# Hybrid decoder layer on one core: stick-breaking sticks alternate between two heads, values' product on two column tiles

## What is computed

```python
z = jnp.einsum('bhqd,bhkd->bhqk', qb, kb) * scale
mask = s_idx[None, :] < t_idx[:, None]
log_beta = jax.nn.log_sigmoid(z)
log_1m = jnp.where(mask, log_beta - z, 0.0)
log_a = log_beta + lax.cumsum(log_1m, axis=3, reverse=True) - log_1m
A = jnp.where(mask, jnp.exp(log_a), 0.0)
outs.append(jnp.einsum('bhqk,bhkd->bhqd', A, vb))
```

## Time and profile before

| | |
|---|---|
| median of 3 executions | 1752.62 us (1748.5 to 1753.45) |
| the profiled execution | 1744.41 us, of which the profile's span is 1742.4 us |
| PE busy | 1588.2 us (91%) |
| DVE, ACT, POOL busy | 825.1, 704.8, 510.0 us |
| mix stage, by the trace | about 390 to 862 us of the span |

### The profile page before, as it was taken

One profiled execution on the slowest core, in us unless ns is written; L12 is line 12 of the kernel. 1 busy time (PEld: TensorE's weight loads), 2 busy tenths in 40 slices (PEclk: granted clock), 3 DMA queues, 4 the chain that ended last, 5 costly groups with the idle time before them and its releaser, 6 DMA issues. The chain is left out here.

```text
span 1742.4 us, 37310 instructions
## 1 busy us (share of the span) xinstructions
PE 1588.2 (91%) x15220; PEld 1305.3 (75%) x15220; DVE 825.1 (47%) x1125; ACT 704.8 (40%) x1239; POOL 510.0 (29%) x523
## 2 busy tenths in 40 slices
PE   4999999967999989888928969999999999999997
PEld 3999999965666666666507848888888888888886
DVE  5132442426566665666592433444444444444436
ACT  5243534516667676677633433222222222222213
POOL 6332432413444444344343532111111111111110
PEclk7999999989999999999969979999999999999999
DMA  3334364373413232111232232111111111111104
GB/s 136 109 128 163 122 213 164 122 207 83 106 45 79 51 82 48 45 31 38 62 85 85 97 120 73 49 49 48 48 48 48 48 48 48 48 48 48 60 1 169
DMA packets 79517, 143.91 MB, mean 83 GB/s; under 512 B 15632, under 2 KB 51472, under 8 KB 79392
## 3 DMA queue, kind: packets, MB, share of 16 engines
q1 hardware_dynamic: 75648, 128.26, 23.9%
q10 hardware_dynamic: 3744, 13.85, 2.0%
HBM read 104.51 MB, written 37.57 MB: 82 GB/s over the span
## 5 line engine op out<-in xcount | busy, mean ns | idle before, releaser
L1793 POOL TENSOR_TENSOR ffn_ul<-ffn_relu,ffn_uh 128x512 fp32r<-128x512 f32 x64 | 82.8, 1293 | 575.3 <-ACT ffn_uh L1765 575.3
L1822 DVE TENSOR_TENSOR all_acc<-all_acc,ffn_down 128x512 f32<-128x512 f32 x240 | 161.1, 685 | 121.8 <-PE ffn_down L1869 121.3
L618 PE MATMUL inproj_acc<-xn_xh,inproj_wh 128*128 128x346 f32 (+1 forms) x624 | 207.3, 332 | 8.4 <-DVE inproj_wl L539 8.4
L1861 PE MATMUL ffn_up<-all_mh,ffn_wuh 128*128 128x512 f32 x512 | 200.2, 391 | 10.9 <-DVE ffn_wul L1805 10.9
L618 PE MATMUL inproj_acc<-xn_xh,inproj_wl 128*128 128x346 f32 (+1 forms) x624 | 201.0, 322 | 0.0
L618 PE MATMUL inproj_acc<-xn_xl,inproj_wh 128*128 128x346 f32 (+1 forms) x624 | 200.8, 322 | 0.0
L1861 PE MATMUL ffn_up<-all_mh,ffn_wul 128*128 128x512 f32 x512 | 199.9, 390 | 0.0
L1861 PE MATMUL ffn_up<-all_ml,ffn_wuh 128*128 128x512 f32 x512 | 199.9, 390 | 0.0
L1869 PE MATMUL ffn_down<-ffn_wdh,ffn_uh 128*128 128x512 f32 x512 | 199.7, 390 | 0.0
L1869 PE MATMUL ffn_down<-ffn_wdh,ffn_ul 128*128 128x512 f32 x512 | 199.4, 389 | 0.0
L1869 PE MATMUL ffn_down<-ffn_wdl,ffn_uh 128*128 128x512 f32 x512 | 199.2, 389 | 0.0
(11 more groups left out here) (249 smaller groups left out, 3444.4 us busy)
## 6 DMA issues: line engine op xcount, KB each, us to landing
ffn_raw_u<-in_w_up SPq DMA_DIRECT2D x32, 512.0 KB, 3.3
ffn_raw_d<-in_w_down SPq DMA_DIRECT2D x32, 512.0 KB, 4.2
xn_raw<-in_w_in SPq DMA_DIRECT2D x28, 512.0 KB, 4.5
p_scratch<-inproj_out ACTq DMA_DIRECT2D x26, 520.0 KB, 2.7
chunk_scratch<-inproj_fields SPq DMA_DIRECT2D x4, 2720.0 KB, 9.2
mix_swp<-chunk_scratch SPq DMA_DIRECT2D x68, 128.0 KB, 3.7
inproj_rkv<-p_scratch SPq DMA_DIRECT2D x14, 520.0 KB, 4.6
mix_fld<-chunk_scratch SPq DMA_DIRECT2D x17, 256.0 KB, 3.0
```

What stands on the lines that cost most here:

```text
L618: last = pe.matmul(acc[g][:, 0:size], w[s][:, kt, :], xx[:, kt, col:col + size], start=(kt == 0 and j == 0), stop=(kt == KD - 1 and j == 2))
L1793: pool.tensor_tensor(ul[s][:, f, cols], relu[j % 2][:, :], uh[s][:, f, cols].bitcast(F32), ALU.subtract).then_inc(u_low.sem, 1)
L1822: dve.tensor_tensor(part, part, downs[o % 4][:, :], ALU.add).then_inc(added.sem, 1)
L1861: last = pe.matmul(ups[j][:, :], w[f][:, k, :], xx[:, k, cols], start=(k == 0 and jj == 0), stop=(k == KD - 1 and jj == 2))
```

## The change

- **Order of tasks.** The loop over the two heads is now innermost: block b of head 0, then of head 1. Each head has its own bank for the running sum (`cbs[h]`); the second `zb` bank is given up for it. Scores of task t now wait for the copy of task t-1 (`z_copied`), no longer t-2.
- **Quarters.** PE's order in a tick is scores, rest, values' product, tri; tri runs for t = now - 3. ACT's is exp and ln of t = now - 1, weights of now - 5, copy of z of t = now, then output copy and splits. DVE's is the difference of now - 4, splits, the max of now - 1, the clamp of now. POOL works on now - 1.
- **Values' product.** Made once for both heads of a block, at the second head's tick, in pieces of 128 queries; each piece is two products with a 128x64 stationary operand, one into rows 0 to 63 of `ob`, one into rows 64 to 127. The output copy is one 128x512 copy for both heads.
- **Buffers.** `w` 5 to 3, with two extra 128x128 tiles `wn` for the narrow tasks; `a` 3 to 4.
- **Loads and splits.** By part instead of by head: part 0 is queries 512 up and keys 640 up of both heads, part 1 the rest (`load_part`, `PARTS`, `K_EDGE`). The number of transfers is the same.

```diff
+PARTS = 2
+K_EDGE = (SBW // P + 1) * P
...
-        for h in range(2):
-            for g in reversed(range(GROUPS)):
-                for b in range((g + 1) * SBW // P, -1, -1):
-                    if n in TURN_BEFORE and i + 1 < PAIRS:
-                        ticks.append(Turn(i + 1, TURN_BEFORE.index(n)))
+        for g in reversed(range(GROUPS)):
+            for b in range((g + 1) * SBW // P, -1, -1):
+                if n in TURN_BEFORE and i + 1 < PAIRS:
+                    ticks.append(Turn(i + 1, TURN_BEFORE.index(n)))
+                for h in range(2):
                     ticks.append(Task(i, h, g, b))
                     n += 1
...
-        w = [m.sb(f"w{i}", [P, SBW]) for i in range(5)]
+        w = [m.sb(f"w{i}", [P, SBW]) for i in range(3)]
+        wn = [m.sb(f"wn{h}", [P, P]) for h in range(2)]
...
-        a = [m.sb(f"a{i}", [P, SBW]) for i in range(3)]
-        zb = [m.ps(f"zb{i}") for i in range(2)]
-        cb = m.ps("cb")
+        a = [m.sb(f"a{i}", [P, SBW]) for i in range(4)]
+        zb = m.ps("zb")
+        cbs = [m.ps(f"cb{h}") for h in range(2)]
...
+                    t = now - 1
+                        clamped.wait(act, t)
+                        act.activation(part, part, ACT.Exp).then_inc(exp_done.sem, 1)
+                        exp_done.wait(act, t)
+                        act.activation(part, part, ACT.Ln, bias=1.0).then_inc(ln_done.sem, 1)
+                    yield
+                    t = now - 5
...
+                    t = now
                         z_done.wait(act, t)
                         exponent.wait(act, t - 4)
-                        act.activation(z[t % 4][:, off:], zb[t % 2][:, off:], ACT.Copy, scale=HD ** -0.5).then_inc(z_copied.sem, 1)
+                        act.activation(z[t % 4][:, off:], zb[:, off:], ACT.Copy, scale=HD ** -0.5).then_inc(z_copied.sem, 1)
...
-                        act.activation(o_sb[half, i, g * SBW:(g + 1) * SBW], ob[half, :], ACT.Copy).then_inc(o_copied.sem, 1)
+                        act.activation(o_sb[:, i, g * SBW:(g + 1) * SBW], ob[:, :], ACT.Copy).then_inc(o_copied.sem, 1)
...
-                        z_copied.wait(pe, t - 2)
+                        z_copied.wait(pe, t - 1)
...
-                        pe.matmul(ob[:, off:], v[i % 2][:, b, :], a[t % 3][:, off:], start=first, stop=at(t).last,
-                                  skip_group_check=True).then_inc(pv_done.sem, 1)
+                        for c in range(off, SBW, P):
+                            for h in range(2):
+                                half = slice(h * HD, (h + 1) * HD)
+                                last = pe.matmul(ob[half, c:c + P], v[i % 2][:, b, half], a[(t - 1 + h) % 4][:, c:c + P], start=first,
+                                                 stop=at(t).last, skip_group_check=True)
+                        last.then_inc(pv_done.sem, 1)
+                    yield
+                    t = now - 3
+                    if is_task(t):
+                        soft_low.wait(pe, t)
+                        sums(tri, tri_r, t, at(t).first).then_inc(tri_done.sem, 1)
```

More of the change, by code:

```diff
@@ L895, in _, with before_diagonal @@
             pool.tensor_copy(rest_r[:, :], rest[:, :]).then_inc(tri_set, 1)
[L897 to L898 removed]
+            def before_diagonal(columns, marks):
+                part = columns[:, 0:P]
                 pool.affine_select(out=part, in_=part, compare_op=ALU.is_gt, fill=0.0, base=0,
@@ L911, in _ @@
                     if at(t).diag:
-                        before_diagonal(w[t % 5], off, soft_masked)
+                        before_diagonal(soft_of(t), soft_masked)
                         soft_masked.wait(pool, t)
-                    if SBW - off >= 2 * P:
-                        part, high, low = (x[:, off:] for x in (w[t % 5], wsh[t % 4], wsl[t % 4]))
+                    if not at(t).narrow:
+                        part, high, low = soft_of(t), wsh[t % 4][:, off:], wsl[t % 4][:, off:]
                         rest_done.wait(pool, t - 4)
+                        tri_done.wait(pool, t - 4)
                         pool.tensor_copy(high, part).then_inc(soft_high.sem, 1)
@@ L991, in sticks @@
                     if is_task(t):
+                        part = w[t % 3][:, at(t).off:]
+                        clamped.wait(act, t)
[5 more added lines that the diff above has]
+                    if is_task(t):
+                        part = a[t % 4][:, at(t).off:]
+                        exponent.wait(act, t)
+                        act.activation(part, part, ACT.Exp).then_inc(weights.sem, 1)
+                    yield
+                    t = now
+                    if is_task(t):
                         off = at(t).off
@@ L1020, in sticks @@
                         high_k(*split_at[now - 1])
-                    yield
-                    t = now - 5
-                    if is_task(t):
-                        part = a[t % 3][:, at(t).off:]
-                        exponent.wait(act, t)
-                        act.activation(part, part, ACT.Exp).then_inc(weights.sem, 1)
                     yield
@@ L1312, in sticks @@
                     t = now - 5
-                    if is_task(t):
+                    if is_task(t) and not at(t).last:
                         exponent.wait(pe, t)
-                        if at(t).last:
-                            pe.sem_inc(rest_done.sem, 1)
-                        else:
-                            sums(rest, rest_r, t, at(t).off, False).then_inc(rest_done.sem, 1)
-                    yield
-                    t = now - 4
-                    if is_task(t):
-                        soft_low.wait(pe, t)
-                        sums(tri, tri_r, t, at(t).off, at(t).first).then_inc(tri_done.sem, 1)
+                        sums(rest, rest_r, t, False).then_inc(rest_done.sem, 1)
                     yield
                     t = now - 6
-                    if is_task(t):
+                    if t in second_ticks:
                         i, b, off, first = at(t).i, at(t).b, at(t).off, at(t).first
-                        (weights_masked if at(t).diag else weights).wait(pe, t)
+                        for x in (t - 1, t):
+                            (weights_masked if at(x).diag else weights).wait(pe, x)
                         if first:
```

141 lines of the change are left out of this document (75 added, 66 removed).

## The result

| | before | changed |
|---|---|---|
| median | 1752.06 us (4 runs, 1748.5 to 1753.45) | 1725.17 us (4 runs, 1724.79 to 1725.99) |
| profiled execution, its span | 1744.41, 1742.4 us | 1725.34, 1723.6 us |
| mix stage, us of the span | 390 to 860.3 | 390 to 841 |
| PE busy in it, PE idle in it | 416.40, 53.9 us | 394.66, 56.3 us |

The ratio is 0.9859 [0.9839, 0.9878], -26.9 us where -36 was forecast; between the two profiled executions it is -19.1 (that of before was the fastest of its kernel). The difference of the two spans lies in the mix stage: its ends in the table are 19.3 us apart; what lies behind it takes 1742.4 - 860.3 = 882.1 us before and 1723.6 - 841 = 882.6 after. The table's last row tells where the gain is: PE works 21.7 us less, and is idle no less than before.

The account below looks back on a forecast made before the run. PE was taken as the bound in work, yet idle 54 us in the 472 us mix stage. -31 - 30 + 25 = -36 us: profiled execution 1744.4 to 1708.4, median 1752.6 to 1716.6; range 1683 to 1758.

Parts of the forecast that it names:

- First term: PE's values' product on two column tiles: 46 us instead of 84, plus 7 for tiling changes, -31 us.
- the rival at 1748.6: Values' product: the two column tiles don't overlap, so its term is +11 and the total -4 us; chance 0.19.
- the 70 tiling changes: PE's array switches between full and tiled products 354 times instead of 284, at a mean of 0.1 us: +7 us.
- Second term: Two running-sum banks: PE's waits of `rest` (26.7 us) and before the output copy (3.9 us) go, -30 us.
- the last sentence of the prediction: If PE idles as before and the stage is only 30 us shorter, the two-bank gain was given back: right for wrong reason.
- Third term: One scores bank: PE's scores wait for ACT's copy, held up by exp waiting for the clamp, +25 us.
- an upper bound of 73: One scores bank's greatest cost to PE: 31 us of exposed clamps plus 42 for clamps held up by POOL.
- that ACT did not stand before: ACT's exp directly behind the copy waits for its own task's clamp in 51 of 112 cases: 31 us of new standing.
- The edits at nothing: Stick instructions, fewer `w` buffers, loads and splits cost nothing; tick 0's second split is covered, otherwise a few us once.
- PE alone as the bound: Mix stage: ACT's new waits fit its slack, so the scores bank costs 0: -61 us, 1691.6; chance 0.14.
- The slow ring of the clamp: ACT, DVE and POOL go round one ring, 4.4 us a tick; with all 64 wide ticks +22 us, 1774.6; chance 0.17.
- The slow side: The whole kernel gets slower by more than 5.3 us: chance 0.16, against 0.70 faster and 0.14 the same.

Follow-up runs that it names:

- e2: Changed kernel with the values' product in one piece per head, up to 512 queries, instead of pieces of 128: 1723.94 us, ratio 0.987.
- e3: Changed kernel with all 128-query pieces of head 0 first, then all of head 1, instead of alternating: 1736.24 us, ratio 0.9926.
- e12: Kernel before, one sum bank, PE's order scores, values' product, rest, tri; DVE takes the difference first and the clamp last: 1786.68 us, ratio 1.0221.
- e9: Changed kernel with one more PE wait: tri of task t also waits for the difference of t-1: 1728.95 us, ratio 0.9896.
- e4: Changed kernel without DVE's clamp, exp reading z itself (the minimum with 40 left out): 1711.62 us, ratio 0.9789.
- e5: Kernel before without DVE's clamp, exp reading z itself (the minimum with 40 left out): 1733.74 us, ratio 0.9914.
- e6: Changed kernel with ACT's weights of now - 5 ahead of exp and ln of now - 1: 1727.16 us, ratio 0.9885.
- e8: Changed kernel with ACT's copy of z first in the tick, ahead of exp, ln and weights: 1731.87 us, ratio 0.9897.
- e7: Changed kernel with the first pair's second split at tick 6 and ACT's weights ahead of exp and ln: 1722.55 us, ratio 0.9846.
- e10: Changed kernel with ACT's copy of z first in the tick and the first pair's second split at tick 6: 1727.29 us, ratio 0.9877.
- e1: Changed kernel with the first pair's second split called for at tick 6 instead of tick 0: 1724.28 us, ratio 0.9868.
- e11: Changed kernel run again as it is, on another chip: 1726.13 us, ratio 0.9861.

## Why the prediction was right, and where not

**First term, -31: right in size.** The groups cost 32 x 1.03 + 8 x (0.37 + 0.59 + 0.81) = 47.1 us (0.59 from a 256 wide group, 0.81 on the line between), where 46 were forecast and 84 stood before. The reason given, column tiles that overlap as the slot's tiles do, holds: e2's trace shows records of two products that start and end together, and e3 takes part of the overlap away by order alone and loses 12 us. The Trainium skill's rule ("TensorE: Matmul & The Clock Gate", Part 3, The mechanism), that a load is hidden only behind matmuls of other row groups, would have made a group of 512 cost about 8 x 0.25 = 2.0 us, an estimate from the earlier trace rows. It takes 1.03, so the rule as the prediction quotes it doesn't hold for these 128x64 tiles. The same section leaves a second way open, a load into the background weight buffer; no run here tells whether that is how it goes. This was the rival at 1748.6, and it is out.

PE's busy time fell by only 21.7 us, though. The products alone account for 84 - 47.1 = 37, so some 15 us of other work came in. 7 of them were forecast, for the 70 tiling changes. About 4 are clock, by an estimate from the rows of the first 30 us: 17.88 us at 0.64 lose 6.4 us against full speed, 21.46 us at 0.89 lose 2.4. The 4 or so that remain no run took apart (behind 420 us the clock is 0.99 instead of 1.00), nor was the price of a tiling change measured after.

**Second term, -30: the waits went, the time didn't.** The 26.7 us of `rest` and the 3.9 us before the output copy are gone as said. But PE's idle time of the stage is 56.3 us against 53.9, where 54 - 30 + 25 = 49 was forecast. This is the case that the last sentence of the prediction named: right for the wrong reason, as far as the second bank goes. The rows of PE's waits say where the time went: the scores' waits for the one bank brought back 25.2 + 2.2 = 27.4 us, as the third term had it, the turns at the start 7.9, and the other rows nearly cancel. The reason for the second term holds only in part. e12 brings `rest` down to 6.8 us with one bank, and in e9 the wait that one bank would add for the next tri costs 2.4. As far as these two runs go, it was the places in the tick more than the second bank; the tick of slack for `rest` could not be tested by itself.

**Third term, +25: the size right, with luck, and its cause not borne out.** PE waits 25.2 + 2.2 us for the one scores bank. The 25 was a third of an upper bound of 73, whose parts were all prices of the clamp. One reading under it was wrong: the median of 428 ns over all clamps mixes four widths, and does not say that a 512 wide clamp was unhindered; of these, 14 of 64 took over 1 us before, and 7 after. The chain from POOL over the clamp to exp to the copy does occur; DVE's, ACT's and PE's timelines show one:

```profile
556.96 1.29 POOL L936 TENSOR_TENSOR mix_wsl<-mix_w,mix_wsh 128x512 fp32r<-128x512 f32 x1
```

```profile
557.24 1.30 DVE L1149 TENSOR_SCALAR mix_w<-mix_z 128x512 f32<-128x512 f32 x1 [1.03 <-ACT mix_z L1026]
```

```profile
558.57 0.63 ACT L1011 ACTIVATE mix_w<-mix_w 128x512 f32<-128x512 f32 x1 [1.36 <-DVE mix_w L1149]
...
560.76 0.59 ACT L1026 ACTIVATE mix_z<-mix_zb 128x512 f32<-128x512 f32 x1
```

```profile
561.41 0.50 PE L1322 MATMUL mix_zb<-mix_qh,mix_ks 128*128 128x512 f32 x1 [0.79 <-ACT mix_z L1026]
```

The clamp began at 557.24 beside POOL's low part (556.96 + 1.29 = 558.25) and took 1.30 us; exp stood 1.36 us for it, the copy ended at 560.76 + 0.59 = 561.35, and the scores had stood 0.79 us. The rule of the Trainium skill on the shared ports ("SBUF — State Buffer", Who interferes with whom) fits in kind, as with the earlier trace rows: the clamp is held up until POOL's part ends. It isn't met to the letter, since the clamp ended 558.54 - 558.25 = 0.29 us behind POOL's part, in the earlier trace rows 0.15, where a 512 wide one takes 0.43 unhindered; times on POOL are rough. But this is not what sets the total. The clamp of 512 takes 615 ns on the mean in both kernels; without it both orders gain, 12 us (e4) and 15 us (e5); and with half of ACT's wait removed and the clamps shorter (e6), PE waits as long as in the changed kernel. The step that failed here is "that ACT did not stand before": ACT stood 61.0 us at its copies, behind the difference. The change moved these waits to exp (65.4), and e8 moves them back to the copy (101.4). Which resource sets the pace of this ring (POOL's two parts, DVE's three operations, the 4 buffers of z, or the scores bank) stays open. More z buffers were not tried, nor a second scores bank beside the two sum banks.

**The edits at nothing: this step failed.** "The second is now called for in tick 0, which PE's and ACT's wait for the first chunk covers": it doesn't. ACT stood 6.89 us for the second load, the first copy of z came 5.4 us later than before, and PE's turns waited 7.9 us. With the split at tick 6 the first copy is early again in all three traces, and the medians are 4.6 us lower twice (e7 under e6, e10 under e8), though e1 alone doesn't show it. The low clock at the start is not the split's doing alone: it was 0.64 here, but 0.73 in e1 and 0.56 in e7. The prediction had named the price of a missing cover, "a few us once", and then not put it into the sum.

That makes half of the 9 us between forecast and result in the medians. Held against the traces, from which the sum was made, the forecast is further off: 1708.4 against 1725.34, 17 us. Of these, 9 are PE's work (-21.7 where -31 was forecast) and 7 its idle time (+2.4 where -5 was), in which the turns' 7.9 us lie. That the medians are nearer is luck: the profiled execution of before was its fastest, 8 us under the median.

**The other rivals.** PE alone as the bound (1691.6) is out: PE idles 56 us. The slow ring of the clamp (1774.6) is out too: it would have made the stage 22 us longer than the 472 of before, and it ran 451, 3.4 us a tick; and the clamps' mean didn't rise. The slow side was the less likely, but e12 shows how near it lies: DVE's two exchanged quarters and the moved product cost 39 us.

## What to carry to other kernels

A wait that a change removes is not yet time: ask for the ring that it lies on, and what on that ring is late next; compare the engine's idle time over the stage, not the row that vanished. Products whose stationary operand is half a tile wide are worth pairing on two column tiles, with neighbouring products on different tiles; in these runs the size of the pieces was free. A wait at the first tick of a stage may have no cover, so it goes into the sum. Where idle time grows, look at the clock as well: e12 has the products of the kernel before, and PE's busy time grew with its idle time.

## What was not expected of the hardware

Two 128x64 column tiles overlapped fully with 512 wide pieces, one head's product behind the other's (1.01 us for what alternating 128 wide pieces do in 1.03). With eight records of one tile ahead of eight of the other they overlapped in part, 1.51 us.

The same kernel's executions lay between 1722.87 and 1732.36 us. In e1 and e11 a longer execution had a lower mean granted clock, 0.966 to 0.958 over the whole span. In the changed kernel's two profiled ones the granted clock of the stage's first 30 us was 0.64 and 0.57, PE having stood there some 8 us for ACT's copies of the turns, and the later one ended its stage 5.9 us later with nearly the same waits. A single execution of this kernel can't tell a change of 5 us.

The changed kernel also runs at a slightly lower clock than the one before: a mean of 0.962 to 0.964 in the four executions of the result, 0.964 to 0.968 in the 32 executions of before beside the experiments.
